# Pairwise state updates in 32-row tiles, no meta tokens in queries and output gates, and an unrolled TensorE program, in an mLSTM-Conformer layer on one core

## What is computed

```python
def mlstm_chunk(carry, blk):
    C0, n0, m0 = carry                    # C0: value x key, 256 x 256 a head
    q, k, v, it, lf = blk
    ...
    p = w_intra * jnp.einsum('bhtd,bhsd->bhts', q, k)
    num = jnp.einsum('bhts,bhse->bhte', p, v) + w_state[..., None] * jnp.einsum('bhed,bhtd->bhte', C0, q)
    den = jnp.sum(p, axis=-1) + w_state * jnp.einsum('bhd,bhtd->bht', n0, q)
    h = num / jnp.maximum(jnp.abs(den), jnp.exp(-m))[..., None]
    ...
    C1 = w_last[..., None, None] * C0 + jnp.einsum('bhs,bhse,bhsd->bhed', ws, v, k)
    n1 = w_last[..., None] * n0 + jnp.einsum('bhs,bhsd->bhd', ws, k)
    return (C1, n1, m_last), h
```

## Time and profile before

| | |
|---|---|
| median of 3 runs | 1296.65 us (1294.78 to 1299.86) |
| the profiled execution: time | 1296.17 us |
| its span, first to last instruction | 1294.4 us |
| mean granted clock of TensorE | 0.991 |
| busy: TensorE, VectorE, ScalarE, GpSimd | 1275.3, 742.5, 388.8, 19.9 us |
| read from and written to memory | 100.89 and 14.21 MB |

### The profile page before, as it was taken

One profiled execution on the slowest core, in us unless ns is written; L12 is line 12 of the kernel. 1 busy time (PEld: TensorE's weight loads), 2 busy tenths in 40 slices (PEclk: granted clock), 3 DMA queues, 4 the chain that ended last, 5 costly groups with the idle time before them and its releaser, 6 DMA issues.

```text
span 1294.4 us, 20276 instructions
## 1 busy us (share of the span) xinstructions
PE 1275.3 (99%) x7944; PEld 1204.9 (93%) x7944; DVE 742.5 (57%) x1327; ACT 388.8 (30%) x534; POOL 19.9 (2%) x37
## 2 busy tenths in 40 slices
PE   7999999999999999999999999999999999999997
PEld 7999999999999999999999998899899889989986
DVE  5633379786968696889846455444234233323453
ACT  4442133214311431131216623233113212312431
POOL 1000000000000000020000000000000000000000
PEclk8999999999999999999999999999999999999999
DMA  8252162316221622253232246111222222222221
GB/s 230 68 152 73 50 169 67 88 59 163 75 79 55 166 76 78 73 96 78 82 82 66 66 130 196 33 50 65 98 82 66 82 81 67 81 79 74 90 82 49
DMA packets 160540, 116.38 MB, mean 90 GB/s; under 512 B 13887, under 2 KB 148247, under 8 KB 160450
## 3 DMA queue, kind: packets, MB, share of 16 engines
q1 hardware_dynamic: 139122, 94.58, 25.8%
q10 hardware_dynamic: 21328, 20.55, 5.0%
HBM read 100.89 MB, written 14.21 MB: 89 GB/s over the span
## 4 chain that ended last, share of the span: by engine, by line
PE 95%; ACT 2%; issue 2%; DVE 1%; DVEq 0%; POOLq 0%; POOL 0%
PE out L363 43%; PE out L1550 29%; PE bank L1550 19%; PE bank L1545 4%; ACT CV L616 1%; PE out L371 1%; DVE WK L1019 0%; ACT WH L314 0%; ACT L648 0%; ACT L616 0%; ACT GH L616 0%; DVE XL L1016 0%; ACT WK L648 0%; DVE XL L413 0%; ACT XH L616 0%
## 5 line engine op out<-in xcount | busy, mean ns | idle before, releaser
L318 DVE TENSOR_TENSOR WL<-ST,WH 128x1024 fp32r<-128x1024 f32 x137 | 167.7, 1224 | 169.8 <-ACT WH L419 100.6
L363 PE MATMUL out<-XH,WH 128*128 128x328 f32 (+1 forms) x1024 | 242.9, 319 | 2.4 <-issue 2.4
L363 PE MATMUL out<-XH,WL 128*128 128x328 f32 (+1 forms) x1024 | 240.9, 317 | 0.0
L363 PE MATMUL out<-XL,WH 128*128 128x328 f32 (+1 forms) x1024 | 240.4, 316 | 0.0
L1019 DVE SCALAR_TENSOR_TENSOR CV<-WK,cwu,CV 128x512 f32 (+1 forms) x480 | 227.2, 544 | 0.4
L363 PEld LDWEIGHTS out<-XH,WH 128*128 128x128 f32 x1024 | 173.9, 190 | 3.5 <-issue 2.5
L363 PEld LDWEIGHTS out<-XH,WL 128*128 128x128 f32 x1024 | 174.5, 190 | 2.0 <-issue 1.3
L363 PEld LDWEIGHTS out<-XL,WH 128*128 128x128 f32 x1024 | 174.5, 189 | 0.9
L1016 DVE TENSOR_TENSOR WK<-WK 128x640 f32<-128x640 f32 (+7 forms) x78 | 64.7, 835 | 109.9 <-ACT WK L982 100.2
L1550 PE MATMUL bank<-WK 128*128 128x16 f32 (+8 forms) x752 | 126.9, 311 | 0.0
L1550 PE MATMUL out<-XH,WL 128*128 128x320 f32 (+2 forms) x512 | 119.9, 310 | 0.0
(11 more groups left out here) (213 smaller groups left out, 1608.8 us busy)
## 6 DMA issues: line engine op xcount, KB each, us to landing
ST<-in_w_in SPq DMA_DIRECT2D x65, 512.0 KB, 4.0
ST<-in_w_ff SPq DMA_DIRECT2D x64, 512.0 KB, 3.9
WK<-in_state_mlstm_C ACTq DMA_DIRECT2D x32, 256.0 KB, 4.1
o_C_sample<-WK ACTq DMA_DIRECT2D x32, 256.0 KB, 2.2
WK<-in_x_prompt SPq DMA_DIRECT2D x8, 512.0 KB, 6.2
ST<-in_w_branch_m SPq DMA_DIRECT2D x8, 512.0 KB, 3.8
ST<-in_w_branch_c SPq DMA_DIRECT2D x8, 512.0 KB, 3.7
ST<-in_w_out SPq DMA_DIRECT2D x8, 512.0 KB, 4.2
```

The lines of the kernel that those rows point to most:

```text
L318: dve.tensor_tensor(WL[:, par % 2, :, :], ST[:, par % NSTAGE, :, :], WH[:, par % 2, :, :].bitcast(F32), ALU.subtract).then_inc(sem("w_lo"), 1)
L363: last = pe.matmul(out[s][:, h, 0:H], w[:, s, kk, :], x[:, kk, h * H:(h + 1) * H], start=(m < 2), stop=(m >= len(ms) - 2))
```

## The change

- Tiles 2, 3, 6 and 7 of a head (queries and output gates) use the 320-column halves; the operations on q, the gates and the numerators leave out the meta columns, and the meta chunk's scores and numerator go. Its keys, values and state update stay.
- The samples are paired: 0 and 2, 4 and 6, 1 and 3, 5 and 7. A 32-row block holds two samples, of which a mask (`pmask`, even or odd) lets one through; a pair is two neighbouring 32-row blocks, one updating into B7 and one into B6. Eight updates in slots 0, 2, 4, 6, 8, 10, 11, 12 become four pairs in slots 2, 4, 8, 12. As B6 is shared with the numerators, pairs wait for the last numerator's copy and numerators for the last pair's two updates by VectorE.
- Stores and loads of the states go two at a time, and transposes and state products move to other slots.
- On TensorE alone the loops over heads and over the MLP's parts are written out.

```diff
+FRAMES_ONLY = (2, 3, 6, 7)
...
-S_SLOT = {0: 0, 2: 1, 4: 2, 6: 3, 8: 4, 10: 5}
+S_SLOT = {2: 1, 4: 2, 6: 3, 8: 4, 10: 5}
 NUM_SLOT = {1: 0, 3: 1, 5: 2, 7: 3, 9: 4, 13: 5}
-UPD_SLOT = {0: 0, 2: 1, 4: 2, 6: 3, 8: 4, 10: 5, 11: 6, 12: 7}
-TR_SLOT = {0: 0, 1: 1, 2: 2, 3: 3, 5: 4, 6: 5, 8: 6, 10: 7}
-INT_SLOT = {1: 0, 2: 1, 3: 2, 4: 3, 6: 4, 7: 5, 9: 6, 11: 7}
+PAIR_SLOT = {2: 0, 4: 1, 8: 2, 12: 3}
+TR_SLOT = {0: 0, 1: 1, 2: 2, 3: 3, 6: 4, 7: 5, 9: 6, 10: 7}
+INT_SLOT = {1: 0, 2: 1, 3: 2, 4: 3, 7: 4, 8: 5, 10: 6, 11: 7}
+SAMPLE = [0, 2, 4, 6, 1, 3, 5, 7]
...
-STORE_SLOT = {_s + 1: _b for _s, _b in UPD_SLOT.items()}
-LOAD_SLOT = {_s + 2: _b + C0RING for _s, _b in UPD_SLOT.items() if _b + C0RING < NB}
+STORE_SLOT = {_s + 1: _p for _s, _p in PAIR_SLOT.items()}
+LOAD_SLOT = {_s + 2: _p + 2 for _s, _p in PAIR_SLOT.items() if _p < 2}
+def pairs_done(s):
+    return 2 * sum(x < s for x in PAIR_SLOT)
...
-        return HALF if n.base < N_GM0 else HALF2
+        return HALF if n.base < N_GM0 and (n.base - N_HEADS0) % PER_HEAD not in FRAMES_ONLY else HALF2
...
-                evac(n + 2, two(q[:, 0, :]))
+                evac(n + 2, two(q[:, 0, NMETA:T]))
...
                     if s in STORE_SLOT:
-                        c1_store(i, STORE_SLOT[s])
+                        for x in range(2):
+                            c1_store(i, 2 * STORE_SLOT[s] + x)
                     if s in LOAD_SLOT:
-                        c0_load(i, LOAD_SLOT[s])
+                        for x in range(2):
+                            c0_load(i, 2 * LOAD_SLOT[s] + x)
...
                 dve.wait_ge(sem("consts"), 4)
+                V.link(tt(pmask[:, :], bmask[:, 0:2], bmask[:, 2:4], ALU.add))
+                V.link(tt(pmask[:, :], pmask[:, :], bmask[:, 4:6], ALU.add))
+                V.inc(tt(pmask[:, :], pmask[:, :], bmask[:, 6:8], ALU.add))
...
+                V.inc(dve.tensor_scalar(wsp[:, :], pmask[:, :], colH[:, 3 * SMP + 1:3 * SMP + 2], None, ALU.mult))
...
-                    dve.tensor_scalar(vws[:, u % 2, :], vtok[:, SMP, :], wsb[:, c:c + 1], None,
-                                      ALU.mult).then_inc(sem("vws"), 1)
+                    r0 = 64 * (c % 2)
+                    dve.tensor_scalar(vws[r0:r0 + 64, u % 2, 0:DH], vtok[r0:r0 + 64, SMP, 0:DH],
+                                      wsp[r0:r0 + 64, c // 2:c // 2 + 1], None, ALU.mult).then_inc(sem("vws"), 1)
...
                 if kind == "D":
-                    slot = c % C0RING
-                    dve.wait_ge(sem(f"c0_in{slot}"), 16 * ((NB // C0RING) * i + c // C0RING + 1))
-                    stt(c0[:, slot, :, :], c0[:, slot, :, :], colH[:, 23 + c:24 + c], psum, ALU.mult,
-                        ALU.add).then_inc(sem("c1"), 1)
+                    for x in range(2):
+                        b = 2 * c + x
+                        slot, col = b % C0RING, 23 + SAMPLE[b]
+                        dve.wait_ge(sem(f"c0_in{slot}"), 16 * ((NB // C0RING) * i + b // C0RING + 1))
+                        stt(c0[:, slot, :, :], c0[:, slot, :, :], colH[:, col:col + 1],
+                            (B7, B6)[x][:, :].rearrange("p (j e) -> p j e", j=2), ALU.mult,
+                            ALU.add).then_inc(sem("c1"), 1)
...
+                if s == 11 or s in NUM_SLOT:
+                    wait(pe, "c1", NB * i + pairs_done(s))
                 if s == 11:
-                    pe.wait_ge(sem("num"), 6 * i + NPC)
+                    pe.wait_ge(sem("num"), 5 * i + NPC - 1)
                     mm(B6[0:NB, 0:DH], wsb[:, :], ktok[:, SMP, :]).then_inc(sem("t_n1"), 1)
-                if s in NUM_SLOT:
+                if NUM_SLOT.get(s, 0) > 0:
...
-                            pe.wait_ge(sem("c1"), NB * i + UPDATES[u - 1][1] + 1)
+                            pe.wait_ge(sem("c1"), NB * i + 2 * UPDATES[u - 1][1] + 2)
...
+                        if s == 12:
+                            pe.wait_ge(sem("n1"), i + 1)
+                        else:
+                            wait(pe, "num", 5 * i + sum(x < s and c_ > 0 for x, c_ in NUM_SLOT.items()))
                         for e in range(2):
-                            ins = mm(B7[:, e * DH:e * DH + DH], w[:, e * P:e * P + P], ktok[:, SMP, :])
+                            for x in range(2):
+                                rows = slice(64 * (c % 2) + 32 * x, 64 * (c % 2) + 32 * x + 32)
+                                ins = mm((B7, B6)[x][:, e * DH:e * DH + DH], w[rows, e * P:e * P + P],
+                                         ktok[rows, SMP, :])
                     ins.then_inc(sem("t_upd"), 1)
...
-                        gemm(pe, n + r, XH, XL)
+                        xh, xl = (XH2, XL2) if r in FRAMES_ONLY else (XH, XL)
+                        gemm(pe, n + r, xh, xl)
...
-            head(0)
-            with pe.Fori(1, HEADS) as i:
+            for i in range(HEADS):
                 head(i)
...
-            ffn(0)
-            with pe.Fori(1, DFF // D - 1) as c:
+            for c in range(DFF // D - 1):
                 ffn(c)
```

More of the change, by code:

```diff
@@ L805, in head @@
                     rows_exp()
-                evac(n + 3, two(q[:, 1, :]))
+                evac(n + 3, two(q[:, 1, NMETA:T]))
                 if not first:
@@ L824, in head @@
                     exp_weights(i)
-                evac(n + 6, two(so[:, 0, :]), ACT.Sigmoid)
+                evac(n + 6, two(so[:, 0, NMETA:T]), ACT.Sigmoid)
                 if first:
@@ L830, in head @@
                 hi(n + 8)
-                evac(n + 7, two(so[:, 1, :]), ACT.Sigmoid)
+                evac(n + 7, two(so[:, 1, NMETA:T]), ACT.Sigmoid)
                 if first:
@@ L843, in head @@
                         copy(wk(off["c0t"], 512), B4[:, :], "c0t_ready")
-                    if s in NUM_SLOT and NUM_SLOT[s] < NPC:
+                    if 0 < NUM_SLOT.get(s, 0) < NPC:
                         numer(i, NUM_SLOT[s])
@@ L1145, in epilogue_norm @@
             def epilogue_norm(i):
[L1147 to L1153, removed]
+                den, mean, var = num[:, 1:6, DH], mv[:, 1:6, 0], mv[:, 1:6, 1]
@@ L1154, in epilogue_norm @@
+                emin = colH[:, 5:18:3]
+                dve.wait_ge(sem("num"), 5 * i + 5)
+                V.link(stt(sm[:, 19:24], den, -1.0, den, ALU.mult, ALU.max))
+                V.inc(tt(sm[:, 19:24], sm[:, 19:24], emin, ALU.max))
+                for c in range(1, 6):
+                    V.inc(dve.bn_aggr(mv[:, c, :], bst[:, c, :]))
                 V.wait()
-                V.link(dve.reciprocal(sm[:, 36:42], sm[:, 18:24]))
-                V.link(tt(sm[:, 18:24], var, sm[:, 36:42], ALU.mult))
@@ L1166, in epilogue_norm @@
-                dve.wait_ge(sem("hn"), 6 * i + 6)
+                V.link(dve.reciprocal(sm[:, 19:24], sm[:, 31:36]))
+                V.link(tt(sm[:, 37:42], sm[:, 37:42], sm[:, 19:24], ALU.mult))
+                V.link(stt(sm[:, 43:48], mean, -1.0, sm[:, 37:42], ALU.mult, ALU.mult))
+                for c in range(1, 6):
+                    dve.tensor_scalar(num[:, c, 0:DH], num[:, c, 0:DH], sm[:, 36 + c:37 + c],
+                                      sm[:, 42 + c:43 + c], ALU.mult, ALU.add).then_inc(sem("hn"), 1)
@@ L1168, in epilogue_gate @@
+                dve.wait_ge(sem("hn"), 5 * i + 5)
             def epilogue_gate(i):
@@ L1194, in scores_weights @@
                 dve.wait_ge(sem("bc_in"), 16 * (i + 1))
-                for c, (c_, L) in enumerate(CHUNKS):
+                for c in range(1, 6):
+                    c_, L = CHUNKS[c]
                     mask = maskd if c == SMP else maskc
@@ L1308, in head @@
                         c_, L = CHUNKS[c]
-                        dve.wait_ge(sem("t_s"), 6 * i + c + 1)
-                        wait(dve, "t_num", 6 * i + c - 1)
-                        if c == 0:
+                        dve.wait_ge(sem("t_s"), 5 * i + c)
+                        wait(dve, "t_num", 5 * i + max(c - 2, 0))
+                        if c == 1:
                             dve.wait_ge(sem("wt"), i + 1)
@@ L1316, in head @@
                                 (kind == "U" and NUM_SLOT.get(s) == UPDATES[u][1]) or
-                                (kind == "D" and UPD_SLOT.get(s) == UPDATES[u][1])):
+                                (kind == "D" and PAIR_SLOT.get(s) == UPDATES[u][1])):
                             update(i, u)
@@ L1331, in head @@
                             ALU.add).then_inc(sem("n1"), 1)
-                    if s in NUM_SLOT and NUM_SLOT[s] in (0, 1, 2, 3, 4):
+                    if 0 < NUM_SLOT.get(s, 0) < NPC:
                         stats(i, NUM_SLOT[s])
@@ L1661, in slot @@
                 if s in S_SLOT or s in INT_SLOT or NUM_SLOT.get(s, NPC) < NPC:
-                    wait(pe, "p_ready", 6 * i + sum(x < s for x in S_SLOT))
+                    wait(pe, "p_ready", 5 * i + sum(x < s for x in S_SLOT))
                     wait(pe, "ct_ready", NPC * i + sum(x < s and c < NPC for x, c in NUM_SLOT.items()))
@@ L1708, in slot @@
```

(4 more changed lines are left out.)

52 lines of the change are left out of this document (23 added, 29 removed).

## The result

The changed kernel took 1287.08 us, median of five runs (1286.79 to 1289.76), against 1296.65 before (five runs by then, 1294.65 to 1299.86): a ratio of 0.993, 95% interval 0.9911 to 0.995. The profiled execution took 1286.92 us, 9.25 under that of before.

A forecast was written before the change was run, and what follows sets the result against it. TensorE was taken as the bound, busy for 1275.3 of 1294.4 us. From 1296.17, -3.2 - 3.3 - 2.5 - 6.9 + 6.4 = -9.5 gave 1286.7, stated as 1287 us; own range 1282 to 1292, 8-in-10 range 1280 to 1299.

The forecast's parts named there:

- Narrower tiles, meta chunk: Sixteen query and gate tiles at 0.20 us each, -3.2 us; meta score and numerator dropped in four heads, -3.3 us.
- Pairs: Sixteen two-sample state updates on TensorE, 1.3 us a pair against 1.73 for two single updates: -6.9 us.
- starts keep the program's order ... five lengths: Inside a pair, only neighbouring passes of different tiles overlap, so eight passes take five lengths of 0.217, 1.09 us.
- rival (3): Full concurrency inside the pairs: 0.89 + 0.2 us each, -10.2 us in all, so 1283 us; chance 0.16.
- I take 0.2 for a pair: Cost of changing the shape of TensorE's array use at each pair, put at 0.2 us.
- Rival (1): The pairs' row tiles do not run together: a pair costs 1.73 + 0.2 us, total 1296.8; chance 0.17.
- The new wait: Before slot 13's product, TensorE waits for VectorE's two updates to free B6: 1.6 us a head, +6.4 us.
- Cover of the other pairs: Behind the other pairs, 16 projection matmuls (2.4 us) cover the 1.8 us VectorE needs, so no wait there.
- Unrolling: TensorE's two issue waits at the head loop's back edges go, -2.5 us; nothing charged for the MLP's loop.
- Clock: TensorE's half-clock stretches behind slot 1, three heads of four, about 1.5 us each; change put at 0.
- I count as many as before: Half-clock stretches: shorter slot 1 speaks for fewer, pairs and slot 13's wait for new ones; net 0 us.
- Rival (2): The clock falls at all 16 pair slots: 13 more falls at 1.5 us, +19.5, total 1306; chance 0.07.

The follow-up runs named there:

- e5: Changed kernel with only the narrower tiles undone (tiles 2, 3, 6, 7 back to 328 columns a half): 1290.35 us, ratio 0.9956 to before.
- e3: Changed kernel with a pair's two loops swapped, so one sample's matmuls precede the other's: 1288.97 us, ratio 0.9949 to before.
- e6: Changed kernel with only the pairing undone (eight 128-row updates a head in the slots of before): 1286.04 us, ratio 0.9923 to before.
- e2: Changed kernel with both samples of a pair on one row tile (second sample's state computed wrongly): 1304.7 us, ratio 1.0069 to before.
- e1: Changed kernel with the last pair moved from slot 12 to slot 10: 1276.28 us, ratio 0.9849 to before.
- e7: Changed kernel with VectorE taking B6's sample first, slot 13 waiting for that update alone, stores for both: 1286.08 us, ratio 0.9922 to before.
- e4: Changed kernel with only the unrolling undone (TensorE's loops over heads and MLP parts back): 1295.48 us, ratio 0.9998 to before.
- e9: Kernel before the change with only TensorE's two loops unrolled: 1290.43 us, ratio 0.9959 to before.
- e8: Changed kernel with the last pair in slot 10 and TensorE's two loops back: 1280.24 us, ratio 0.9874 to before.

## Why the prediction was right

The time was 1287 foreseen and 1287.08 found. The terms behind it held within 0.6 us each, but for the clock. That the sum agrees to 0.1 us is luck: the clock (+1.5, put at 0) and head 2 (+0.4, in no term) are cancelled by terms that gained more and by 1.0 us outside all of them, which is not explained.

- **Narrower tiles, meta chunk.** -3.2 and -3.3 were -3.15 and -3.6, from pitches of the trace of before. e5 shows the first by itself (3.2 in its tiles); of the second, the score was 0.38 where 0.3 was put.
- **Pairs.** 1.3 us a pair was 1.26, but by errors that cancel. The step "starts keep the program's order ... five lengths" failed: the row tiles take their passes independently, so there are four lengths, and e3 shows that the program's order inside a pair doesn't matter. What came true is the mechanism of rival (3), the full concurrency, at the forecast's price: that is luck. The strict order that the Trainium skill's page "TensorE: Matmul & The Clock Gate" has in "Part 3: Packing small matmuls" is not what these starts show. The step "I take 0.2 for a pair" was too small: four starts 0.217 apart would be 0.87, and 0.39 more goes into the change of shape. Against slot 4 of e6, 0.09 of it stand ahead of the first pass, 0.10 in the first distance and 0.20 behind the last pass. That is the 0.39 which the earlier trace rows gave for slot 1; the 16-row passes there stand together too, as one visit, so halving it for a pair was wrong. Rival (1) is what e2 built, and it is out.
- **The new wait.** 1.6 a head was 1.7: from the pair's last pass at 281.911 to the product at 283.944 there are 2.03 us for 0.217, less 0.1 of the shape's end that hides in it. Its price by itself was right, but not all that it brought (see the clock). e1 and e7 show that it is VectorE's two updates, and e6 that it takes the gain of all the pairs.
- **Cover of the other pairs.** No wait stands behind the pairs of slots 2, 4 and 8; stores and loads two at a time left none either.
- **Unrolling.** -2.5 was -2.7 at the edges, but the term was priced for the kernel before alone. Beside the new wait it was worth 8.4 us (e4), and even in before 5.3 (e9), as the clock came with it. For the MLP's loop nothing was put, and nothing came (e4).
- **Clock.** "I count as many as before" was nearly right in number, four for three, and wrong in place: behind slot 1 there were two instead of three, and two came behind slot 13's wait. The forecast had named both, and let them cancel. The Trainium skill, page "TensorE: Matmul & The Clock Gate", "Why this matters for your kernels", ties a fall to idle gaps: the two behind the wait had a gap ahead of them (TensorE busy for 1.86 of 3.40 us ahead of 412.40), though a shorter one (1.66 us) than the page's row names; the two behind slot 1 had none (busy for 3.40 of 3.40 us ahead of 228.10), as in the earlier trace rows. What the forecast missed is that the wait's price includes falls. Over all traces a fall stands at slot 13 or right behind it in 16 of the 20 heads with a wait of 1.65 to 1.74 us there (the changed kernel, e2 to e5), and in none of the four with 1.0 us (e7) or the 20 with no wait before slot 13's product (before, e1, e6, e8, e9). So of the 10.8 us that e1 gained, 6.9 are the wait and some 3 the two falls behind it. The falls behind slot 1 differ from one trace to the next and are not shown to follow the wait.
- **Rival (2).** The six more falls that were to outweigh the gain are 9.0 us against 9.5; it takes seven. No falls came with the pairs by themselves: e1 has all sixteen pairs and one fall.

## What to carry to other kernels

Before an operation's output moves into a bank that another product needs, look for the next use of that bank and count the matmuls in between: here 16 projection matmuls covered VectorE's 1.8 us in three slots and none did in the fourth, and two slots' distance was worth 10.8 us. A bottleneck engine's stall had a second price here, in the clock behind it and in a branch that followed it, so measure a removed wait on the chip and don't only subtract its length. Small fp32 updates on 32 rows do run two at a time, but each visit to them costs about 0.4 us beside its passes here, so put as many passes as possible into one visit.

## What the hardware did that was not expected

- Passes on two row tiles start in twos in both orders of the program that were tried: 7 ns apart in the changed kernel and 13 in e3.
- A loop's back edge on TensorE costs 1.0 to 1.5 us of idle time when nothing holds the engine just ahead of it (e8) and 3.3 us when a semaphore wait stands in the slot before it (e4). That the sequencer, held at the wait, then has no matmuls queued to cover the branch is a reading of these rows, not shown.
- The clock's falls move with the rest of the program. With slot 1 unchanged they were three in before and one in e9, which differ in TensorE's loops alone, and single runs of a kernel lie 0.9 to 5.3 us apart, not by the granted clock alone (e1: 1273.77 and 1276.28 us, both at 0.995).
